# Mixing stage of a two-layer trunk: decays split around the inverse blocks, copies reordered, modulation groups moved

## What is computed

```
for layer in (0, 1):
    mod = silu(c) @ ada_w + ada_b          # 6 x 1024 shifts, scales, gates, one column for latents, one for context
    h   = rmsnorm(x) * (1 + scale) + shift
    r, k, v, B, C, x, wl, al, gl, q, K, V, gates = h @ w_in
    conv  = B * dwconv3(C * x)
    decay = exp(-exp(-softplus(-(w0 + tanh(wl) @ w2)) - 0.5));  a = sigmoid(a0 + al @ a2);  g = sigmoid(gl) @ g2
    kk    = k * rsqrt(sum(k*k per head));  k_d = k * (1 + (a-1)*k_a);  b_d = kk * a
    for t (both directions):               # the recurrence, per head of 64
        S = S*decay_t - (S kk_t) b_t + v_t k_t;   y_t = S r_t
    rwkv  = (groupnorm(y) + bonus(r, k_d) * v) * g
    x += mod * (merge(conv, rwkv, attention(q, K, V), gates) @ w_o)
    x += mod * conv_ffn(rmsnorm(x) ...)
```

## Time and profile before

| | us |
|---|---|
| median of three runs | 3057.61 (3052.55 to 3057.68) |
| profiled execution | 3056.1, span 3054.3 |
| PE busy | 2882.4 (94%) |
| DVE busy | 1276.9 (42%) |
| ACT busy | 753.3 (25%) |
| POOL busy | 51.6 (2%) |
| mean granted clock of PE | 0.979 |
| mixing, layer 0 (78 to 840): PE busy | 714.97 of 762 |
| attention and tail, layer 0 (840 to 1392): PE busy | 540.66 of 552 |
| norm and mixing, layer 1 (1860 to 2520): PE busy | 590.08 of 660 |

### The profile page before, as it was taken

The page is one execution under the profiler, slowest core; times in us unless marked ns, Lnnn a source line. Parts: engine busy times, 40 slices in busy tenths (PEclk is TensorE's granted clock), DMA queues, the critical chain, the costliest instruction groups (busy, mean ns, idle before and its releaser), DMA issues.

```text
span 3054.3 us, 57161 instructions
## 1 busy us (share of the span) xinstructions
PE 2882.4 (94%) x25177; PEld 1745.3 (57%) x25177; DVE 1276.9 (42%) x2585; ACT 753.3 (25%) x1465; POOL 51.6 (2%) x76
## 2 busy tenths in 40 slices
PE   7899999999999999999999998898888999999999
PEld 3455555555644445444444443666666667788887
DVE  2565555665332222023444112555566643322551
ACT  3233332333222222002111003333334322221110
POOL 1000000000000000000000000000000000000000
PEclk9999999999999999999999999999999999999999
DMA  7212222211233443222222223222211114444554
GB/s 243 74 39 63 71 61 66 66 52 50 72 104 87 106 110 102 78 76 71 76 76 76 75 74 95 80 67 72 73 46 46 53 45 125 111 118 136 154 149 120
DMA packets 499845, 264.24 MB, mean 87 GB/s; under 512 B 42848, under 2 KB 493744, under 8 KB 499088
## 3 DMA queue, kind: packets, MB, share of 16 engines
q1 hardware_dynamic: 497872, 251.57, 29.1%
q0 software_dynamic: 1728, 9.03, 0.8%
HBM read 255.31 MB, written 5.24 MB: 85 GB/s over the span
## 4 chain that ended last, share of the span: by engine, by line
PE 88%; ACT 5%; DVE 2%; issue 2%; DMA 2%; SPq 0%; ACTq 0%; DVEq 0%
PE psum L453 57%; PE psum L1025 7%; PE psum L474 2%; PE psum L647 2%; PE psum L750 1%; DMA strips<-in_w_in_dram 1%; PE psum L870 1%; ACT arena L1342 1%; PE psum L764 1%; PE psum L733 1%; PE psum L848 1%; PE psum L715 1%; PE psum L800 1%; PE psum L858 1%; PE psum L789 1%
## 5 line engine op out<-in xcount | busy, mean ns | idle before, releaser
L453 PE MATMUL psum<-hT,strips 128*128 128x512 f32 (+1 forms) x3968 | 1462.6, 518 | 48.8 <-ACT arena L1417 27.4
L453 PEld LDWEIGHTS psum<-hT,strips 128*128 128x128 f32 x3968 | 739.1, 193 | 579.7 <-issue 488.1
L1025 PE MATMUL psum<-arena,strips 128*128 128x512 f32 (+1 forms) x704 | 227.6, 486 | 0.6 <-DVE arena L2203 0.6
L1025 PEld LDWEIGHTS psum<-arena,strips 128*128 128x128 f32 x704 | 133.7, 190 | 93.5 <-issue 83.5
L453 PE MATMUL psum<-arena,strips 128*128 128x512 f32 (+1 forms) x512 | 167.9, 486 | 3.0 <-DVE done L2090 3.0
L1573 ACT COPY arena<-psum 128x512 f32<-128x512 f32 (+1 forms) x88 | 42.2, 479 | 388.9 <-PE psum L453 375.4
L453 PEld LDWEIGHTS psum<-arena,strips 128*128 128x128 f32 x512 | 97.1, 190 | 71.5 <-issue 60.7
L1705 DVE TENSOR_SCALAR arena<-arena 128x512 f32<-128x512 f32 (+1 forms) x88 | 37.0, 421 | 238.9 <-ACT arena L1573 238.8
L2055 DVE SCALAR_TENSOR_TENSOR arena<-arena,psum 128x512 f32<-128x512 f32 (+1 forms) x32 | 17.8, 555 | 269.1 <-PE psum L453 269.1
L1867 DVE TENSOR_TENSOR arena<-psum,tables 128x1024 f32<-128x1024 f32 x48 | 58.5, 1220 | 117.0 <-PE psum L647 117.0
L1973 DVE TENSOR_TENSOR arena<-psum,arena 64x256 f32<-64x256 f32 x112 | 47.3, 422 | 111.4 <-PE psum L750 111.2
(11 more groups left out here) (251 smaller groups left out, 3293.1 us busy)
## 6 DMA issues: line engine op xcount, KB each, us to landing
strips<-in_w_in_dram SPq DMA_DIRECT2D x158, 512.0 KB, 4.2
strips<-in_ffn_up_dram SPq DMA_DIRECT2D x88, 512.0 KB, 3.8
strips<-in_ada_w_dram SPq DMA_DIRECT2D x80, 512.0 KB, 3.9
strips<-in_ffn_down_dram SPq DMA_DIRECT2D x32, 512.0 KB, 4.1
arena<-in_ada_w_dram SPq DMA_DIRECT2D x4, 2048.0 KB, 15.5
strips<-in_w_in_dram SPq DMA_DIRECT2D x32, 256.0 KB, 3.8
strips<-in_a_out_w_dram SPq DMA_DIRECT2D x16, 512.0 KB, 4.4
strips<-in_rwkv_out_w_dram SPq DMA_DIRECT2D x16, 512.0 KB, 5.6
```

The source lines that it names most:

```text
L453: ins = mm(s.o[:, first:T], strip[:, b, k, :], rhs[:, k, first:T], k == 0, k == KT - 1)
L1025: ins = mm(s.o[:, lo:T], strip[:, b, j, :], hid[:, k, lo:T], k == 0, k == FT - 1)
```

## The change

- PE: g's product leaves `decays` and becomes `decay_gate`. In the loop the order is key sums, the two decay products, `through_inverse`, a fill of 2, `decay_gate`, a drain of PE that releases the low-rank weights (before: the first matmul of `through_inverse` did). `diagonal_blocks(i + 1)` moves from the head of tile i + 1 to ahead of `outputs(i)`. `ada_pick` moves behind a pair product and a fill. Some fills change (6 to 8, 6 to 4, 2.4 to 2.3 in layer 1; in the last tile the full ones are used).
- ACT: `through_inverse(i)` ahead of `decays(i + 1)`; `conv_gate` ahead of both `powers`. Table sets are loaded by name: the set with ln and exp ahead of a norm or the key norm, the one with exp and tanh behind it, and the first ahead of `head_inverse`.
- DVE: `state_in(0)` ahead of `decays(i + 1)`, `half_step` ahead of the taps of r, `conv_taps` ahead of the last `state_in`, `keys(0)` earlier in layer 1's last tile.
- Modulation: the four groups (1, 8..11) move from layer 1's mixing to behind branch(2, n), n = 0, 2, 4, 6, of layer 0's tail; their picks follow gate(2, n + 2). DVE adds the biases of all of layer 1's modulation at one place.

```diff
-        MIX_ADA = [[(0, 4 + i) for i in range(KT)], [(1, 8 + i) for i in range(4)] + [None] * 4]
+        MIX_ADA = [[(0, 4 + i) for i in range(KT)], [None] * KT]
+        TAIL_ADA = [{0: (1, 8), 2: (1, 9), 4: (1, 10), 6: (1, 11)}, {}]
@@ PE
+                def decay_gate(i):
                     s = take(A, "g", l, i)
                     one(PS[:, BANK_A[s.b], lo:T], lw[:, 2, :], low[:, 2, lo:T]).then_inc(s.full[0], 1)
@@ PE, tail of attend
+                        if n - 1 in TAIL_ADA[l]:
+                            ada_pick(A, *TAIL_ADA[l][n - 1], part_att)
                         branch(2, n)
+                        if n in TAIL_ADA[l]:
+                            ada_group(*TAIL_ADA[l][n])
@@ PE, mix
                 fill(steps, everything)
+                diagonal_blocks(0)
                 for i in range(KT):
-                    diagonal_blocks(i)
                     turn_hats(0, i)
...
                     if lo and ahead:
-                        fill(steps, 6)
+                        fill(steps, 8)
                     if i > 0:
                         head_var(i - 1)
                     half_step(i)
+                    pair_products(1, 0, i)
+                    fill(steps, 10 if wide or not ahead else 4)
                     if MIX_ADA[l][i]:
                         ada_pick(A, *MIX_ADA[l][i], part_mix)
-                    pair_products(1, 0, i)
-                    fill(steps, 10 if wide else 6)
                     corners(i)
...
                     if ahead:
                         key_sums(i + 1)
                         decays(i + 1)
-                    through_inverse(i, ahead)
+                    through_inverse(i)
+                    if ahead:
+                        fill(steps, 2)
+                        decay_gate(i + 1)
+                        pe.drain().then_inc(lr.free, 1)
                     for c in range(NCH):
                         state_in(c, i)
                         if c > 0:
-                            fill(steps, 4 if wide else 2.4)
+                            fill(steps, 4 if wide else 2.3)
...
                     fill(steps, everything)
+                    if ahead:
+                        diagonal_blocks(i + 1)
                     outputs(i)
@@ ACT
             def norm(n, lo):
+                logs()
                 s = await_slot("norm", n)
...
+                exps_and_tanhs()
...
                 def key_norm(i):
+                    if i < 2:
+                        logs()
...
+                    exps_and_tanhs()
...
                     if ahead:
                         key_norm(i + 1)
-                        decays(i + 1)
                     through_inverse(i)
                     if ahead:
+                        decays(i + 1)
+                        conv_gate(i + 1)
                         powers(0, i + 1)
-                        conv_gate(i + 1)
                         powers(1, i + 1)
@@ DVE
                     bonus(i)
+                    state_in(0, i)
                     if ahead:
                         decays(i + 1)
                     steps = hats(i + 1) if ahead else iter(())
                     for c in range(NCH):
-                        state_in(c, i)
+                        if c > 0:
+                            state_in(c, i)
...
+                        if ahead and c == NCH - 2:
+                            t = conv_taps(i + 1)
```

More of the change, by code:

```diff
@@ L721, in bonus_sums, with through_inverse @@
                     one(PS[:, BANK_P[s.b], lo:T], tab["heads"], th[:, 2, lo:T]).then_inc(s.full[0], 1)
-                def through_inverse(i, ahead):
+                def through_inverse(i):
                     pe.wait_ge(*slots["t10", l, i].freed)
@@ L734, in through_inverse @@
                                          TLR[r, 8 * h + 4 * d + m].rearrange("p b t -> p (b t)"), EE[r, k0:3, c // 4, d, h, c % 4, :])
-                                if ahead and (m, d, h, p) == (0, 0, 0, 0):
-                                    ins.then_inc(lr.free, 1)
                         ins.then_inc(s.full[0], 1)
@@ L955, in mix @@
                 decays(0)
+                decay_gate(0)
                 pe.drain().then_inc(lr.free, 1)
                 fill(steps, everything)
+                diagonal_blocks(0)
                 for i in range(KT):
@@ L974, in mix @@
                     half_step(i)
+                    pair_products(1, 0, i)
+                    fill(steps, 10 if wide or not ahead else 4)
                     if MIX_ADA[l][i]:
                         ada_pick(A, *MIX_ADA[l][i], part_mix)
-                    pair_products(1, 0, i)
-                    fill(steps, 10 if wide else 6)
                     corners(i)
                     pair_products(1, 1, i)
-                    fill(steps, 6 if wide else 4)
+                    fill(steps, 6 if wide or not ahead else 4)
                     below_left(i)
                     value_products(i)
-                    fill(steps, 4 if wide else 3)
+                    fill(steps, 4 if wide or not ahead else 3)
                     corner_below(i)
                     bonus_sums(i)
-                    fill(steps, 4 if wide else 3)
+                    fill(steps, 4 if wide or not ahead else 3)
                     if ahead:
@@ L1146, in _ @@
                     load_attention_out(l, n)
+                    if n in TAIL_ADA[l]:
+                        load_ada(*TAIL_ADA[l][n])
                 for k in range(KT):
@@ L1242, in _, with logs, exps_and_tanhs @@
             act.wait_ge(s_tab, 16)
+            def logs():
+                act.preload_act_table_set("natural_log_exp_and_others")
+            def exps_and_tanhs():
+                act.preload_act_table_set("exp_and_others")
             def await_slot(*key):
@@ L1374, in head_inverse @@
                 def head_inverse(i):
+                    if i < KT - 1:
+                        logs()
                     s = filled("var", i)
@@ L1513, in attend @@
                         gate(2, n)
+                        if n - 1 in TAIL_ADA[l]:
+                            ada_part(*TAIL_ADA[l][n - 1], part_att)
+                            ada_raw(*TAIL_ADA[l][n - 1])
                 centre(0, "r", 0, lo)
@@ L2060, in late_mods @@
                 def late_mods():
-                    for u in MIX_ADA[l]:
-                        if u:
-                            dve.wait_ge(*slots[("pick", *u)].freed)
                     if l == 0:
+                        dve.wait_ge(*slots[("pick", *MIX_ADA[0][KT - 1])].freed)
                         biased(0, 2 * KT, 6 * KT)
                         halved_gate(0)
-                    else:
-                        biased(1, 4 * KT, 6 * KT)
                 def attend():
@@ L2133, in mix @@
                     spread_blocks(i, t)
+                    half_step(i)
                     if ahead:
                         taps(0, "r", i + 1, lo, 0)
-                    half_step(i)
                     masked_pairs(1, 0, i)
@@ L2155, in mix @@
                                 gated(i + 1)
-                        if not ahead and c == (6 if lo else 3):
+                        if not ahead and c == (4 if lo else 3):
                             keys(0)
@@ L2165, in mix @@
                             next(steps, None)
+                        if ahead and c == NCH - 2:
+                            t = conv_taps(i + 1)
                     if ahead:
-                        t = conv_taps(i + 1)
                         taps(2, "v", i + 1, 0, 3)
@@ L2208, in ffn @@
                         setup(1)
-                        for u in ATT_ADA[0]:
-                            dve.wait_ge(*slots[("pick", *u)].freed)
-                        biased(1, 0, 4 * KT)
+                        dve.wait_ge(*slots[("pick", *TAIL_ADA[0][6])].freed)
+                        biased(1, 0, 6 * KT)
                         halved_gate(1)
```

## The result

| | before | changed |
|---|---|---|
| median | 3057.64 us (4 runs) | 3112.1 us (3111.45 to 3114.39, 4 runs) |
| ratio to before, 95% interval | | 1.0181 (1.0164 to 1.0198) |
| profiled execution, span | 3056.1, 3054.3 | 3114.39, 3112.6 |
| PE busy, PE idle | 2882.4, 171.9 | 2918.0, 194.6 |
| mean granted clock of PE | 0.979 | 0.966 |

A forecast was written before the change was run, and what follows sets the result against it. The matmul engine, busy 2882.4 of 3054.3 us, was taken as the bound. Terms +35 (layer 0), -2 (layer 1), 0 (groups) and -3.4 (tables) made +30 us on 3056.1, stated as 3086 us, range 3046 to 3104.

The forecast's parts named there:

- the hold: Layer 0 mixing, seven tiles: PE's in1 waits a new 3.3 us for VectorE's state_out(0), behind the later tanhs.
- the clock term: Layer 0, behind the wait at in1: half-rate dense matmuls add 1.4 us a tile (ends 0 and 2.0).
- part 4: Inverse blocks before tanhs in layer 1: +0.6 us a tile, +4.2 in seven; with inverse and last-tile gains, -2 us.
- The groups: Four modulation groups moved to layer 0's tail: net 0; -17 if the tail hides it, +5 if attn_out loads are slower.
- Rival D: The forecast itself, with its clock and modulation-group terms between their ends: 3066 to 3104 us; chance 0.68.
- The drain: PE, behind g's product: 0, covered by the wait for decay0's bank; uncovered, up to 14 x 0.3 = 4 us.
- The norms: Table sets loaded by name: the load moves from between Ln and Exp to behind Exp, -3.4 us.
- part 3: Diagonal blocks ahead of outputs: +0.35 us a tile in layer 0; PE's inverse wait in layer 1 gone, -5.2.
- C's copy ahead of powers: Layer 0 mixing: x's wait for C adds 0.36 us a tile; powers(0) waiting for C costs 0.
- A: Faster: in1 isn't held, as state_out(0) comes less than 1.5 + 0.3 us later; 3031 us, chance 0.17.
- B: in1 is held, but no half-rate stretch (-10) and the tail hides the strips (-17): 3059 us, chance 0.09.
- C: Compiler still puts a table load ahead of each Exp, 1.28 us more 14 times: +18, 3104 us, chance 0.06.

The follow-up runs named there:

- e1: Changed kernel with VectorE's state_out(0) moved ahead of decays(i + 1) and the first hats: 3050.54 us, ratio 0.9986 to the kernel before.
- e3: Changed kernel with the four modulation groups back in tiles 0 to 3 of layer 1's mixing: 3111.34 us, ratio 1.0189 to the kernel before.
- e2: Changed kernel with ScalarE's four tanhs ahead of the inverse blocks' copies again, g's copy still behind them: 3064.74 us, ratio 1.0025.
- e4: Kernel before with only the table sets loaded by name: 3054.66 us, ratio 1.0005.
- e7: Kernel before with only the diagonal blocks of tile i + 1 ahead of outputs(i): 3058.35 us, ratio 1.0001.
- e8: Kernel before with only C's copy ahead of powers(0): 3056.17 us, ratio 0.9995.
- x2: e2 with a dense fill between blocks 1 and 2, x gated behind state_in(4), diagonals ahead in layer 1 only: 3028.63 us, ratio 0.9904.
- e5: Changed kernel with a fill of 6 columns in place of 4 behind out0 in layer 0: 3084.05 us, ratio 1.0090.
- h1: Changed kernel with VectorE's state_out(0) two hats steps earlier, still behind the running sums: 3098.81 us, ratio 1.0138.

## Why the prediction was right or wrong

**Right: the place and the length of the hold.** Forecast 3.3 us at in1 in layer 0, measured 3.18 or 3.19 in all seven tiles; out0 0.6 against 0.77, x 0.65 against 0.68, B 0.26 against 0.20, y's bank 0.65 against 0.58; in layer 1 in1 2.4 against 1.66 to 2.39, x 1.45 against 1.15, out0 1.05 against 1.48. The idle time added in layer 0 was forecast as 7 x 3.57 = 25 us and measured as 21.3. e1 shows that the chain named (tanhs, sums, state_out(0), in1) is the cause: one step moved on VectorE removes it.

**Wrong: the clock term, and with it the size.** The prediction put 1.4 us a tile (ends 0 and 2.0) on half-rate matmuls behind the hold, from two stretches in which a single wait had been followed by one slow group. PE's busy time in layer 0 grew by 30.4 us, 4.3 a tile, so the term is short by 20 us. From out0 to out3, right behind the hold, the excess over full rate is 22.2 us, 3.2 a tile: the slow stretch lasts longer than the one group that was read. In four tiles it begins before x's wait, in the other three with it, and it runs into the fill behind it. The other 8 us lie elsewhere in the tiles, behind waits that the kernel before also has; why they grew isn't shown. e1 took 26.9 us of the 30.4 back by removing the hold.

The rule behind the term, half rate behind a wait "above some 2 us", doesn't hold either. In the kernel before itself a wait of 1.80 us ahead of the corners (L680 at 329.28) is followed, 1.8 us after its end, by six dense products of 4.54 us for 2.84. And of the seven waits of 2.13 us for g's bank in layer 1 five are followed by inverse blocks at full rate (2.62 us), two by slow ones (3.87 and 4.25).

**Wrong: part 4, layer 1.** Apart from the groups and the last tile's fills it forecast -1.0 us for these seven tiles (+4.2 - 5.2). e3, which has the groups back, took 540.2 us for 528.4 before: +11.8, some 4 of them dense work that the last tile's larger fills take ahead of the cut (an estimate from 33 more dense matmuls in the stretch, most of them of the kind that takes 0.13 us). So about +8. The waits at this place came to 0.50, 1.48, 1.15 and 1.66 to 2.39 us, 36.6 in seven tiles for 27.3 before: +9.3, not +4.2. "Over the next four chunks a part is regained" isn't borne out. Half-rate stretches did follow both versions, as it says.

**The groups, by stage.** Their leaving was worth 26.5 us in layer 1 (forecast 9 of work and 12.9 of waits and slow stretches) and cost 23.1 in the middle. The net of 0 is right.

**The range.** The profiled execution grew by 58.3 us, 28 more than forecast: some 17 of them in layer 0, 9 in layer 1's tiles and 3 from the table sets. Rival D's ends don't follow from its terms: 2.0 a tile and +5 for the groups give 3095 at the top, and 0 and -17 give 3059 at the bottom, where it states 3104 and 3066.

**Right, and measured.** The groups: net 0 (e3). The drain: none seen where a wait covers it, 0.26 us where it isn't covered (e2).

**Right in part.** The norms: the 3.4 us of PE's waits went (e4), but the named table sets cost 3.5 us of waits elsewhere, which the prediction put at nothing, so their net is 0. The inverse's wait: 0.9 us are left in the changed kernel, but the diagonals alone leave 3.1 (e7), against part 3: the order on VectorE had to change with it. C's copy ahead of powers: alone it costs 8.9 us of waits in layer 0, where powers(0) waits for C and the prediction said 0, and gains 7.8 in layer 1 (e8).

**The rivals.** A (in1 not held) fell at its own point of decision, 5.3 us of delay against 1.8 of cover. B's two parts fell: the slow stretches came, and the strips waited 4.33, 3.28, 3.08 and 1.93 us in the tail where 2.7 each had been forecast. C fell: 28 fewer ScalarE instructions, and Exp directly behind Ln.

## What to carry to other kernels

When one engine's work is put behind another step, follow every queue that the delayed result feeds until you reach something that the critical engine needs soon: here ScalarE's tanhs were for the next tile, but VectorE runs in order, and the current tile's state stood behind them. The cheapest repair was in that queue, not in the one that had been changed. e8 is the same lesson once more, with powers behind C's copy on ScalarE. A wait was best filled with independent dense work here (x2), rather than moved, and a price for it is incomplete without PE's busy time: compare the busy sums of the same stretch at the same number of matmuls, and over all tiles. One tile can mislead: e5's tile 1 ran on at full rate where five of its seven didn't.

## What the runs showed of the hardware

Half-rate stretches can cost as much as the wait in front of them: in layer 0 the hold at in1 is 22.3 us in seven tiles, and the matmuls from out0 to out3 took 22.2 us more than at full rate; over the whole of these tiles 21.3 us of added idle time came with 30.4 of added busy time for the same matmuls.

The length of a wait doesn't say which rate follows. Waits of 2.33 us (e5, layer 0) were followed by full rate in two tiles and half rate in five, 1.86 (h1) by full rate in four and half rate in three, 2.40 (e2, layer 0) by full rate in one and half rate in six, 2.79 (e2, layer 1) by full rate in four and half rate in three. 3.18 us was followed by half rate in all seven, and so was, once, a wait of 1.80 us ahead of the corners in the kernel before. These runs give no rule for it.

Small matmuls slow down as well: groups of eight 64-column products took 0.69 or 0.70 us for 0.45. A table load took 1.28 us in every case, and the next instruction started within 0.02 us of its end where it waited for nothing else.
